# The low half of every weight unit made in two subtractions, and a wait at each product's middle tile

## The reference

```python
def first_block(x, ...):
    h = rmsnorm(x, norm_mix_g)
    q, k, v, xr, gr, g_attn, g_rnn = split(h @ w_in)
    attn = diff_attention(q, k, v, ...)            # 8 heads, two softmaxes each, causal, bias by distance
    rnn = rg_lru_branch(xr, gr, ...)               # conv of 4 taps, two gates per block of 128, scan, gelu
    merged = sigmoid(g_attn) * (attn @ w_proj_attn) + sigmoid(g_rnn) * (rnn @ w_proj_rnn)
    x = x + merged @ w_out
    x = x + square(relu(rmsnorm(x, norm_mlp_g) @ w_up)) @ w_down          # 4096 wide
def second_block(x, mem, ...):
    h = rms_norm(x, mix_norm_g)
    # three branches: short convolution, attention with forget gates, banded attention with a sink
    x = x + (gated sum of the three branches @ w_branch) @ w_mix_out
    x = x + cross_attention(rms_norm(x), rms_norm(mem))                    # 4 heads, 256 memory rows
    x = x + (silu(rms_norm(x) @ w_gate) * (rms_norm(x) @ w_up)) @ w_down  # 2816 wide
    return rms_norm(x, final_norm_g)
```

## Time and profile before

| | |
|---|---|
| median of 3 runs | 2035.38 us (2035.09 to 2038.58) |
| the profiled execution | 2037.93 us, of which the span is 2036.1 us |
| PE matmul | 1944.5 us busy, 95% of the span, 9015 matmuls |
| DVE | 1075.8 us, 53% |
| ACT | 496.6 us, 24% |
| POOL | 1240.7 us, 61%, 1018 instructions |
| mean granted TensorE clock | 0.989 of full speed |
| chain that ended last | PE 75%, DVE 18%, issue 3%, ACT 3% |

### The profile page before, as it was taken

How to read it: one execution, slowest core, us unless ns; L and a number is a source line. 1 busy time by engine, 2 the same in 40 slices (tenths; PEclk the granted TensorE clock), 3 DMA queues, 4 the chain that set the end, 5 groups by cost and what they waited for, 6 DMA issues and landing times.

```text
span 2036.1 us, 23483 instructions
## 1 busy us (share of the span) xinstructions
PE 1944.5 (95%) x9015; PEld 1594.0 (78%) x9015; DVE 1075.8 (53%) x1514; ACT 496.6 (24%) x998; POOL 1240.7 (61%) x1018
## 2 busy tenths in 40 slices
PE   8888887999999999999999999999999989999997
PEld 6666666888888888888888778888779878888886
DVE  5677758998364131227866675333655563223134
ACT  4444443432122010012233333100222221001012
POOL 6333326878766776676633444776667587676662
PEclk9999998999999999999999999999999999999999
DMA  5221102333333333333312322333433233333321
GB/s 161 72 60 56 53 25 78 99 107 104 95 94 96 101 93 94 102 94 94 92 46 59 78 63 69 98 93 88 124 94 105 72 104 95 102 94 95 102 78 57
DMA packets 341169, 177.39 MB, mean 87 GB/s; under 512 B 14453, under 2 KB 338203, under 8 KB 341060
## 3 DMA queue, kind: packets, MB, share of 16 engines
q1 hardware_dynamic: 338834, 173.14, 29.5%
q10 hardware_dynamic: 2226, 2.76, 0.6%
HBM read 173.75 MB, written 2.13 MB: 86 GB/s over the span
## 4 chain that ended last, share of the span: by engine, by line
PE 75%; DVE 18%; issue 3%; ACT 3%; POOL 0%; ACTq 0%; DMA 0%; SPq 0%; DVEq 0%; POOLq 0%
PE bank L650 22%; PE bank L654 22%; PE bank L652 22%; PE bank L772 2%; PE bank L749 1%; DVE aPR L1710 1%; DVE aPR L1712 1%; DVE IT L1818 1%; DVE XC L1799 1%; DVE HS L1828 1%; DVE HS L1829 1%; DVE aPR L1702 1%; PE bank L738 1%; PE bank L718 1%; DVE ACC L1823 1%
## 5 line engine op out<-in xcount | busy, mean ns | idle before, releaser
L615 POOL TENSOR_TENSOR WL<-RAW,WH 128x1024 fp32r<-128x1024 f32 (+3 forms) x331 | 812.9, 2456 | 27.5
L650 PE MATMUL bank<-HH,WH 128*128 128x512 f32 x1560 | 622.7, 399 | 14.6 <-DVE SQ L1670 7.4
L654 PE MATMUL bank<-HH,WL 128*128 128x512 f32 x1560 | 617.1, 396 | 0.0
L652 PE MATMUL bank<-HL,WH 128*128 128x512 f32 x1560 | 614.3, 394 | 0.0
L611 POOL TENSOR_TENSOR gate<-gate 128x1 f32<-128x1 f32 x331 | 89.2, 270 | 737.8 <-PE bank L654 687.9
L650 PEld LDWEIGHTS bank<-HH,WH 128*128 128x128 f32 x1560 | 295.3, 189 | 79.0 <-issue 20.6
L612 POOL TENSOR_SCALAR WH<-RAW 128x1024 fp32r<-128x1024 f32 (+3 forms) x331 | 344.6, 1041 | 0.0
L652 PEld LDWEIGHTS bank<-HL,WH 128*128 128x128 f32 x1560 | 295.4, 189 | 60.1 <-issue 4.2
L654 PEld LDWEIGHTS bank<-HH,WL 128*128 128x128 f32 x1560 | 294.7, 189 | 60.4 <-issue 1.9
L1869 DVE TENSOR_TENSOR X<-X,bank 128x512 f32<-128x512 f32 x80 | 54.9, 687 | 202.7 <-PE bank L654 202.7
L650 PE MATMUL bank<-UH,WH 128*128 128x512 f32 x256 | 99.9, 390 | 0.3
(11 more groups left out here) (407 smaller groups left out, 3205.0 us busy)
## 6 DMA issues: line engine op xcount, KB each, us to landing
RAW<-in_w_in SPq DMA_DIRECT2D x107, 512.0 KB, 3.7
RAW<-in_w_up SPq DMA_DIRECT2D x32, 512.0 KB, 3.9
RAW<-in_w_down SPq DMA_DIRECT2D x32, 512.0 KB, 3.9
RAW<-in_w_ffn_gate SPq DMA_DIRECT2D x22, 512.0 KB, 3.7
RAW<-in_w_ffn_up SPq DMA_DIRECT2D x22, 512.0 KB, 3.7
RAW<-in_w_xkv SPq DMA_DIRECT2D x16, 512.0 KB, 3.8
RAW<-in_w_ffn_down SPq DMA_DIRECT2D x16, 512.0 KB, 3.5
RAW<-in_w_proj_attn SPq DMA_DIRECT2D x8, 512.0 KB, 3.8
```

The lines of the kernel that those rows point to most:

```text
L615: nc.gpsimd.tensor_tensor(WL[:, s, 0:k, :], RAW[:, s, 0:k, :], WH[:, s, 0:k, :].bitcast(F32), ALU.subtract).then_inc(S_[f"unit_cut{s}"], 1)
L650: mm(psum[s][:, 0:n], WH[:, s, k, :], hi(k), start=(k == 0), stop=False)
L652: mm(psum[s][:, 0:n], WH[:, s, k, :], lo(k), start=False, stop=False)
L654: last = mm(psum[s][:, 0:n], WL[:, s, k, :], hi(k), start=False, stop=(k == tiles - 1))
```

## The change

POOL makes WL of a unit in two subtractions, one over the first half of its row tiles and one over the second, each counting `unit_cut` up by one. So a cut counts two. SP waits for both halves before it loads the slot anew, and a product waits for the first half at its start and for the second at its middle tile. `rnn_gates` and the unit of the merge with code of its own wait for both at the start.

```diff
--- before.py
+++ after.py
@@ -421,7 +421,7 @@
             def load(name, it, j, pieces):
 
                 s, c = units.use(name, it, j)
-                sp.wait_ge(S_[f"unit_cut{s}"], c - 1)
+                sp.wait_ge(S_[f"unit_cut{s}"], 2 * c - 2)
                 for p0, pn, k0, src, c0 in pieces:
                     kn, cn = src.shape[1], src.shape[2]
                     sp.dma_start(RAW[p0:p0 + pn, s, k0:k0 + kn, c0:c0 + cn], src).then_inc(S_[f"landed{s}"], 16)
@@ -565,7 +565,7 @@
         @block.gpsimd
         def _(pool):
             for s in range(SLOTS):
-                pool.sem_inc(S_[f"unit_cut{s}"], 1)
+                pool.sem_inc(S_[f"unit_cut{s}"], 2)
                 pool.sem_inc(S_[f"hi_made{s}"], 1)
             nc.gpsimd.memset(ident[:], 0.0).then_inc(once("ident_clear")[0], 1)
             nc.gpsimd.memset(ones[:], 1.0).then_inc(once("ones_made")[0], 1)
@@ -612,8 +612,9 @@
                 nc.gpsimd.tensor_scalar(WH[:, s, 0:k, :], RAW[:, s, 0:k, :], 1.0, 1.0, ALU.mult, ALU.mult
                                         ).then_inc(S_[f"hi_made{s}"], 1)
                 pool.wait_ge(S_[f"hi_made{s}"], c)
-                nc.gpsimd.tensor_tensor(WL[:, s, 0:k, :], RAW[:, s, 0:k, :], WH[:, s, 0:k, :].bitcast(F32),
-                                        ALU.subtract).then_inc(S_[f"unit_cut{s}"], 1)
+                for half in (slice(0, k // 2), slice(k // 2, k)):
+                    nc.gpsimd.tensor_tensor(WL[:, s, half, :], RAW[:, s, half, :], WH[:, s, half, :].bitcast(F32),
+                                            ALU.subtract).then_inc(S_[f"unit_cut{s}"], 1)
 
             for name, it, j in units.order:
                 if (name, it, j) == ("mlp", 1, 0):
@@ -642,9 +643,11 @@
 
                 s, c = units.use(name, it, j)
                 tiles = units.tiles[name][j]
-                pe.wait_ge(S_[f"unit_cut{s}"], c)
+                pe.wait_ge(S_[f"unit_cut{s}"], 2 * c - 1)
                 pe.wait_ge(S_[f"taken{s}"], c - 1)
                 for k in range(tiles):
+                    if k == tiles // 2:
+                        pe.wait_ge(S_[f"unit_cut{s}"], 2 * c)
                     if ready:
                         ready(k)
                     mm(psum[s][:, 0:n], WH[:, s, k, :], hi(k), start=(k == 0), stop=False)
```

## The result

The median of four runs is 2019.50 us (2018.36 to 2021.70), against 2036.98 us (2035.09 to 2041.70) in four runs of the kernel before: a ratio of 0.991 (95%: 0.989 to 0.9929), so 0.9% faster. The profiled execution took 2018.36 us, with a span of 2016.6, which is 19.5 us less than before. Of all executions in this document one, of WH in two pieces with WL in four, took 3227.6 us at a mean granted clock of 0.556; it counts in that run's median and in no ratio. The forecast was 2028.9 with a range of 2024.5 to 2037.2: the sign was right and the size less than half.

A forecast was written before the change was run, and what follows sets the result against it. TensorE was taken as the bound, busy 1944.5 of 2036.1 us, with 92 idle us to win apart from lower-clock stretches; terms summed to -6.7 us from 2035.38, giving 2028.7, forecast as 2028.9, range 2024.5 to 2037.2.

The forecast's parts named there:

- first product, to 20 us: TensorE's first product starts after the first half of WL alone, 1.1 us earlier, and keeps the lead: -1.1.
- heads, to 290 us: Attention heads: +0.4 in the first head, 0 for later aPR waits, +0.5 in all at the NMAX waits.
- recurrent start, to 345 us: DVE's long chain gets three turns per cut instead of two; waits for XCL and SQ shrink: -5.0 us.
- Rival 1: POOL does not give up the port between halves, so DVE wins nothing: +1.2 us, 2036.6; chance 0.22.
- Later heads: In heads after the first, TensorE's aPR waits stand behind the unsplit WH and do not change: 0.
- Rival 2: Heads' waits grow by 0.15 us and bring TensorE's clock down: +7.6 us, 2043; chance 0.08.
- the memory's transposes: Three TensorE waits at transposes L1005, behind HL, ACC, then MEML, each grow by 0.15 us: +0.4.
- Rival 3: The seam works, but the recurrent start's order falls otherwise: -1.5 there, total -3.2, 2032.2 us; chance 0.15.
- MGCL: TensorE's wait of 1.4 us for MGCL: one blocked operation ends earlier, less a chain's extra ahead: -0.9.
- FFL: TensorE's wait of 0.7 us for FFL: a single blocked DVE operation ends earlier: -0.6.
- NMAX: Heads' 15 waits for NMAX, after LOGT steps, grow 0 to 0.15 us each: +0.5 in all.
- HL's two waits: TensorE's two waits for HL, 5.3 us: HL ends 0.7 earlier, but ACC waits for the second half: -0.4.

The follow-up runs named there:

- the others alone split: Against the kernel before, WL in two halves in all units but those of the heads and the recurrent stage (270 of 331): 2030.73 us, ratio 0.9956.
- the heads alone: Against the kernel before, WL in two halves only in the first attention's heads and the two units following them (26 of 331): 2032.66 us, ratio 0.9965.

## Why the prediction was wrong

Side by side, prediction and traces are far apart in the heads and in all that follows the recurrent start (us, after less before; the last column sums to the 19.7 of the traces):

| part | predicted | measured |
|---|---|---|
| first product, to 20 us | -1.1 | +0.8 (-1.0, then a clock fall) |
| heads, to 290 us | +0.9 | -6.7 (1.2 of it a clock fall that is missing) |
| recurrent start, to 345 us | -5.0 | -5.2 |
| all that follows | -1.5 | -8.6 |

**The mechanism was right.** VectorE is let in at the seam of two long POOL instructions with no wait between (what the prediction calls giving up the port): LOGT 1.10 and 1.20, HL 1.50 and ACC 1.77. Rival 1 is refuted by every one of these rows. By the Trainium skill (GPSIMD Engine Reference, Instruction dispatch) a Pool instruction does not hold back the next; whatever overlap that gives, it did not keep DVE out here: the halves' records overlap by 0.04 us, and a waiting operation got in.

**The step that failed:** "Later heads: the aPR waits are behind WH, which is not split: 0." Measured: the wait falls from 1.58 to 0.58 us in five heads, and side by side these bring -1.1 each and a sixth -0.5, -6 us. The observation was true (WH is what the operation stood behind, and it is not split), and the conclusion was not: in the earlier trace rows a tie decided at 0.02 us was noticed and made into a rival, while here a tie of 0.01 (88.62 and 88.63) stood in the trace unread. Rival 2 counted the heads' chain 0.15 longer; it became 0.19 shorter, as the hand-over between two DVE operations is hidden when the second waits anyway. The experiments that move POOL by 0.15 and by 0.3 us turn the five heads either way. That the halves turned this tie the good way was luck: nothing in the change aims at it. The chain's 0.19 is read off the trace; that the hidden hand-over makes it is argued.

**A term mis-sized: the places without a wait in the list.** The prediction took TensorE's 92 idle us for all that can be won apart from the clock, and summed only places that show a wait; the units outside heads and recurrent stage brought 9.0 us (0.44%) where it had about -1.5. At a join 0.07 us of idle time stood for 0.3 us lost. Of the 9 us the traces before and after show -0.3 at each of six joins, -1.6 from there to 1233 us, and -2.2 at the memory's transposes, where it had +0.4 (waits 7.1 to 6.3; the first of the three fell from 2.23 to 1.51, and one of three clock falls there is missing). The clock falls are partly chance: the profiled execution with the others alone split shows clock losses in its unsplit heads that the one before does not.

**Right:** the recurrent start, -5.0 predicted. Its two waits fell from 11.3 to 6.4 us, by 4.9; side by side it is -6.7 up to SQ, with a clock fall of before missing, and 1.1 is given back in one behind SQ. VectorE there, which answers to the earlier trace rows:

```profile
299.00 1.82 DVE L1821 SCALAR_TENSOR_TENSOR IT<-IT,XC 128x512 f32<-128x512 f32 x1 [1.88 <-ACT IT L1305]
...
302.31 2.65 DVE L1802 SCALAR_TENSOR_TENSOR XC<-XR,PARAM,XC 128x512 f32<-128x512 f32 x3
305.66 0.91 DVE L1808 TENSOR_TENSOR XCL<-XC,XCH 128x512 fp32r<-128x512 f32 x1 [0.70 <-ACT XCH L1292]
```

IT 1.82 for 2.92, the three XC 2.65 for 5.97, XCL 0.91 for 2.06. The wait for XCL is gone; that for SQ is 6.4, 0.5 above the 5.9 foretold. Rival 3 is out. MGCL -0.9 (predicted -0.9), FFL -0.7 (-0.6), NMAX -0.5 (+0.5), HL's two waits 5.3 and 5.3 (-0.4 predicted), middle tiles 0. POOL's cost was 81 us for the 50 foretold, since the sum left out the turns that DVE takes inside a cut; it stays under POOL's idle time.

**The first product** won the 1.0 us predicted, and the profiled execution lost it in 4 us at the lower clock. In the run with the heads alone its lead of 1.4 us stays. The whole time does not tell it from 0.

**The range** was built from the same sum and its rivals, none of which let the unlisted places gain; the deeper gain that it "leaves out" was the one that came.

## What to carry to other kernels

Where one engine's operation stands for the whole of another's long instruction, as VectorE's here, the length of that instruction is a setting like any tile size: cut it until the engine that holds it has no slack left in its tightest stage (here four pieces, 0.976; eight made POOL the bound in one stage, 0.982), and choose by stage if stages differ. Two pieces help a single waiting operation, or a long chain that meets several cuts; a chain of two needs more. When reading a trace for such a change, look for near ties (issues within 0.2 us of each other) ahead of every wait, not only where durations are long: each tie that turns is worth up to the whole of the rival's instruction. And do not take the list of waits for all that can be won: set two traces side by side, since many short waits do not show in it.

## What was not expected of the hardware

- DVE and POOL take turns by whose instruction was issued first, and 0.01 to 0.2 us decide: 1.57 against 0.77 us for the same operation. An instruction more on POOL made the kernel 0.17% faster.
- Pieces of 256 columns cost POOL 816 ns in the mean and pieces of 128 cost 514, so seven more seams a cut are 8 x 0.514 - 2.54 = 1.6 us more, with DVE's turns inside.
- In some executions the first matmuls stand 0.43 us apart instead of 0.23 for 3 to 4 us, at a granted clock of 0.50, with no link seen to when they start.
- An idle time of 0.07 us ahead of a product can stand for 0.3 us lost, as at the joins.
